# Rotary pairs exchanged by transfers, and attention scores as two split passes

## The reference

```
h = concat([meta_tokens, x]); h = layer_norm(h)          # 528 positions
for l in range(2):
    c_val, c_glu, c_gate, q, k, v, a_gate, r_x, r_gate = split(h @ w_in[l])
    q, k = partial_rotary(q, pos), partial_rotary(k, pos)   # first 16 of 64 dims
    att = sliding_window_sink_attention(q, k, v, sinks)     # window 128, meta keys seen by all
    y = concat([y_conv, att * silu(a_gate), y_lru])
    h = layer_norm(ALPHA * h + y @ w_out[l])

def partial_rotary(x, pos):                  # half = 8
    x1, x2 = x[..., :8], x[..., 8:16]
    return concat([x1 * cos - x2 * sin, x2 * cos + x1 * sin, x[..., 16:]])

s_meta = einsum("bnqkgd,bmkd->bkgnqm", qb, km) * scale     # real queries, 16 meta keys
s_band = einsum("bnqkgd,bnjkd->bkgnqj", qb, k_band) * scale # and 2 blocks of 128 keys
s_mm   = einsum("bqkgd,bmkd->bkgqm", qmg, km) * scale       # meta queries, meta keys
```

## Time and profile before

| | us |
|---|---|
| median of 3 runs (lowest, highest) | 3177.31 (3176.45, 3180.64) |
| the profiled execution's own time | 3175.3 |
| its span | 3173.8 |
| TensorE busy | 3113.7 (98%) |
| VectorE busy | 2194.8 (69%) |
| ScalarE busy | 1557.4 (49%) |
| GpSimd busy | 335.5 (11%) |

### The profile page before, as it was taken

How to read it: one execution, slowest core, us unless ns; L and a number is a source line. 1 busy time by engine, 2 the same in 40 slices (tenths; PEclk the granted TensorE clock), 3 DMA queues, 4 the chain that set the end, 5 groups by cost and what they waited for, 6 DMA issues and landing times.

```text
span 3173.8 us, 59919 instructions
## 1 busy us (share of the span) xinstructions
PE 3113.7 (98%) x23211; PEld 2918.5 (92%) x23211; DVE 2194.8 (69%) x2897; ACT 1557.4 (49%) x2538; POOL 335.5 (11%) x343
## 2 busy tenths in 40 slices
PE   8999999999999999999989999999999999999998
PEld 7899999999999998998889999999998888888898
DVE  7678888888888888786774655566557556556535
ACT  5355555555555555442264554555226455555421
POOL 1000000000000000000001342250000224313000
PEclk9999999999999999999999999999999999999999
DMA  6334444443443435452243222223325322222432
GB/s 209 91 99 108 111 109 113 127 108 103 112 109 102 119 105 180 132 164 93 93 155 98 81 71 71 74 82 122 102 84 169 92 74 80 81 78 70 160 99 88
DMA packets 461729, 342.81 MB, mean 108 GB/s; under 512 B 20505, under 2 KB 451545, under 8 KB 458353
## 3 DMA queue, kind: packets, MB, share of 16 engines
q1 hardware_dynamic: 443712, 296.28, 32.5%
q0 software_dynamic: 8304, 26.92, 2.4%
q10 hardware_dynamic: 9552, 17.37, 1.6%
HBM read 315.04 MB, written 25.46 MB: 107 GB/s over the span
## 4 chain that ended last, share of the span: by engine, by line
PE 75%; DVE 9%; DVEq 5%; DMA 4%; issue 3%; ACT 3%; SPq 0%; ACTq 0%
PE ps L762 13%; PE ps L763 13%; PE ps L764 13%; PE ps L933 5%; PE ps L935 5%; PE ps L936 5%; DVE w_low_blocks L2203 3%; DMA w_raw_blocks<-in_w_in 2%; PE ps L1186 2%; PE ps L1347 1%; PE ps L1345 1%; PE ps L1349 1%; PE ps L768 1%; PE ps L1003 1%; PE ps L769 1%
## 5 line engine op out<-in xcount | busy, mean ns | idle before, releaser
L762 PE MATMUL ps<-x_high,w_high 128*128 128x264 f32 (+3 forms) x2880 | 914.1, 317 | 19.2 <-DVE x_low L2595 10.7
L763 PE MATMUL ps<-x_low,w_high 128*128 128x264 f32 (+3 forms) x2880 | 882.6, 306 | 0.0
L764 PE MATMUL ps<-x_high,w_low 128*128 128x264 f32 (+3 forms) x2880 | 882.4, 306 | 0.0
L2113 DVE TENSOR_TENSOR w_low<-w_raw,w_high 128x1024 fp32r<-128x1024 f32 x308 | 377.7, 1232 | 331.8 <-ACT w_high L1387 317.2
L762 PEld LDWEIGHTS ps<-x_high,w_high 128*128 128x128 f32 x2880 | 544.1, 189 | 51.1 <-issue 21.6
L763 PEld LDWEIGHTS ps<-x_low,w_high 128*128 128x128 f32 x2880 | 544.1, 189 | 28.0 <-issue 3.3
L764 PEld LDWEIGHTS ps<-x_high,w_low 128*128 128x128 f32 x2880 | 542.7, 188 | 25.2
L933 PE MATMUL ps<-x_high_rows,w_high_blocks 128*128 128x256 f32 x1815 | 505.1, 280 | 2.9 <-DVE v_gelu_feature_major L2236 1.9
L935 PE MATMUL ps<-x_low_rows,w_high_blocks 128*128 128x256 f32 x1792 | 496.4, 277 | 0.0
L936 PE MATMUL ps<-x_high_rows,w_low_blocks 128*128 128x256 f32 x1792 | 495.2, 276 | 0.0
L1387 ACT ACTIVATE w_high<-w_raw 128x1024 fp32r<-128x1024 f32 x308 | 324.7, 1056 | 276.3 <-PE ps L764 201.3
(11 more groups left out here) (523 smaller groups left out, 5334.7 us busy)
## 6 DMA issues: line engine op xcount, KB each, us to landing
w_raw_blocks<-in_w_in SPq DMA_DIRECT2D x200, 512.0 KB, 5.1
w_raw<-in_w_in SPq DMA_DIRECT2D x384, 256.0 KB, 3.2
w_raw<-in_w_out SPq DMA_DIRECT2D x224, 256.0 KB, 3.0
w_raw_blocks<-in_w_out SPq DMA_DIRECT2D x24, 512.0 KB, 5.5
residual<-residual_stream ACTq DMA_DIRECT2D x8, 1056.0 KB, 9.7
residual_stream<-y_layer ACTq DMA_DIRECT2D x2, 2176.0 KB, 11.3
x_natural<-in_x SPq DMA_DIRECT2D x4, 1024.0 KB, 9.4
x_feature_major<-x_stage POOLq DMA_DIRECT2D x4, 1024.0 KB, 7.8
```

What stands on the lines that cost most here:

```text
L762: pe.matmul(dst, wh[:, j, kt, wc], x_hi[:, k, tok], start=first, stop=False)
L763: pe.matmul(dst, wh[:, j, kt, wc], x_lo[:, k, tok], start=False, stop=False)
L764: return pe.matmul(dst, wl[:, j, kt, wc], x_hi[:, k, tok], start=False, stop=last)
L2113: dve.tensor_tensor(wl[:, j], raw[:, j], f(wh[:, j]), ALU.subtract).then_inc(lo_ready, 1)
```

## The change

**Rotary.** The product with `rotation` goes, with its constant, for keys and queries. After each copy of queries (or keys) out of PSUM, ScalarE issues four transfers of 8 partitions each, within SBUF, which exchange the rows of each pair into `swapped_pairs`; the sign is now in the sin table. VectorE's `rope` reads that tile in place of PSUM and writes its result to `tmp1` (t = 0) or `c_partial` (t = 1).

**Scores.** For each head, one tile holds the query's high part on the 64 partitions of its own half and its low part on the other half: `q_even_heads` (in the place of the queries) and, for odd heads, `swapped_pairs` (reused). ScalarE writes the high halves (`queries`), VectorE the low halves. The key tile `k_high_low` holds the key's high part on both halves and, in a second plane, its low part on both halves. A score is two float32r passes over the same queries: with the keys' high and with their low plane. ScalarE makes the keys' high parts as before, VectorE 12 subtractions for the low ones between its second and third `low`.

**Order.** TensorE waits for the low halves of the first pair before heads 0 and 1, and of the second pair before heads 2 and 3. VectorE's group loop is written out.

```diff
-        rot = nc.alloc_sbuf_tensor_at("rotation", [P, P], F32, offset=hole + (NM + P) * 4)
-        kz = rr.take("k_zero_padded", [P, 2, 3, NM + 2 * BLK])
+        ks = rr.take("k_high_low", [P, 2, 3, NM + 2 * BLK], F32R)
...
+        swr = rw.take("swapped_pairs", [P, 2, L], F32R)
+        qst = (nc.alloc_sbuf_tensor_at("q_even_heads", [P, 2, L], F32R, offset=big),
+               swr)
+        swap = swr[:].bitcast(F32)
...
+        roped = (t1, cacc)
...
-                pool.dma_start(rot[:], consts[:, K_ROT:K_MASK0]).then_inc(shape_in, 16)
...
-                    def rotate(t):
...
-                        for q, c in enumerate(parts):
-                            last = pe.matmul(ps[:, 4 + 2 * t + q, 0:c.stop - c.start], rot[:], qrw[:, t, c], start=True, stop=True)
-                        last.then_inc(rot_mm, 1)
...
+                    def score(i, n):
+                        q = qst[i % 2][:, i // 2, :]
+                        bank = 4 + n % 2
+                        if n == 0 and i % 2 == 0:
+                            pe.wait_ge(stack_low, 3 * G + i // 2 + 2)
...
-                        last = pe.matmul(ps[:, bank, 0:w], q[:, tq:tq + BLK], kz[:, i % 2, max(n - 1, 0), 0:w],
-                                         start=True, stop=True)
+                        for m in range(2):
+                            last = pe.matmul(ps[:, bank, 0:w], q[:, tq:tq + BLK], ks[:, m, max(n - 1, 0), 0:w],
+                                             start=(m == 0), stop=(m == 1))
...
+                act.wait_ge(zeros_ok, l + 1)
+                act.wait_ge(evac, 2 * (U + O_K2) + 2)
+                for o in (0, PAIR, HD, HD + PAIR):
+                    d = o ^ PAIR
+                    act.dma_start(swap[d:d + PAIR, :, :], krw[o:o + PAIR, :, :]).then_inc(pairs_swapped[0], 16)
...
+                    def swap_pairs(t):
+
+                        act.wait_ge(evac, 2 * V + t + 1)
+                        for o in (0, PAIR, HD, HD + PAIR):
+                            d = o ^ PAIR
+                            act.dma_start(swap[d:d + PAIR, t, cc], qrw[o:o + PAIR, t, cc]).then_inc(pairs_swapped[t], 16)
+
+                    def queries(t):
+
+                        act.wait_ge(rope_done, 2 * G + t + 1)
+                        for h in range(2):
+                            o = h * HD
+                            last = act.activation(qst[h][o:o + HD, t, cc], roped[t][o:o + HD, cc], ACT.Copy)
+                        last.then_inc(stack_high, 1)
...
                     take(V, 0, cols(qrw[:, 0, :]), banks(0))
+                    swap_pairs(0)
                     high(V + 1, 0)
                     values()
                     high(V + 1, 1)
                     keys(0)
-                    keys(1).then_inc(kz_ready, 1)
+                    keys(1).then_inc(stack_high, 1)
                     high(V + 1, 2)
                     take(V, 1, cols(qrw[:, 1, :]), banks(2))
+                    swap_pairs(1)
                     high(V + 1, 3)
+                    queries(0)
+                    queries(1)
...
-                with dve.Fori(0, NKV) as g:
+                for g in range(NKV):
...
-                        dve.wait_ge(rot_mm, 2 * G + t + 1)
-                        dve.tensor_tensor(cols(t1[:]), banks(4 + 2 * t), cols(sin), ALU.mult)
+                        dve.wait_ge(pairs_swapped[t], 64 * (G + 1 + (l + 1 if t == 0 else 0)))
+                        dve.tensor_tensor(r[:, cc], swap[:, t, cc], sin[:, cc], ALU.mult)
...
+                    def queries(t):
+
+                        dve.wait_ge(stack_high, 3 * G + t + 2)
+                        for h in range(2):
+                            o, d = h * HD, (1 - h) * HD
+                            last = dve.tensor_tensor(qst[h][d:d + HD, t, cc], roped[t][o:o + HD, cc],
+                                                     f(qst[h][o:o + HD, t, cc]), ALU.subtract)
+                        last.then_inc(stack_low, 1)
...
+                            for e in range(3):
+                                dve.tensor_tensor(z[:, e, NM:], k[:, NM + e * BLK:NM + (e + 2) * BLK], f(hi_k[:, e, NM:]), ALU.subtract)
+                            for e in range(3):
+                                last = dve.tensor_tensor(z[:, e, 0:NM], k[:, 0:NM], f(hi_k[:, e, 0:NM]), ALU.subtract)
...
-                    lows(V + 1)
+                    low(V + 1, 0)
+                    low(V + 1, 1)
+                    keys()
+                    low(V + 1, 2)
+                    low(V + 1, 3)
                     rope(0)
                     rope(1)
+                    queries(0)
+                    queries(1)
...
-            c[o + q:o + q + half, K_SIN:K_ALL] = np.sin(ang).T
+            c[o + q:o + q + half, K_SIN:K_ALL] = np.sin(ang).T if q else -np.sin(ang).T
```

More of the change, by code:

```diff
@@ L50 @@
 HD = 64
+PAIR = HD // 4 // 2
 NKV = 4
@@ L115 @@
 OUT_ORDER = (6, 7, 0, 1, 2, 3, 4, 5)
-K_IDENT, K_ONES, K_TRI, K_ROT = 0, P, 2 * P, 3 * P
-K_MASK0 = 4 * P
+K_IDENT, K_ONES, K_TRI = 0, P, 2 * P
+K_MASK0 = 3 * P
 K_MASK = K_MASK0 + NM + BLK
@@ L1143, in _ @@
                 unit_half(U + O_K2, fill, COLS[1], (1, 2), hook=parameters)
[L1145 to L1155, removed]
+                unit(U + O_GRP, fill, wide=True, real=(real, real))
                 def group(g, ending=None):
@@ L1160, in group @@
                     A = NH * l + GROUP * g
-                    def rotate(t):
-                        if t == 0:
-                            pe.wait_ge(evac, 2 * V + 2)
-                            pe.wait_ge(k_roped, 2 * (l + 1))
+                    def score(i, n):
[3 more added lines that the diff above has]
+                            pe.wait_ge(stack_low, 3 * G + i // 2 + 2)
+                        if n == 0 and i == 0:
+                            pe.wait_ge(pl_ok, l + 1)
                             pe.wait_ge(r_act, 2 * G)
-                            pe.wait_ge(o_taken, 2 * G)
                             if not real:
                                 pe.wait_ge(mo_ready, 2 * G)
-                        for q, c in enumerate(parts):
-                            last = pe.matmul(ps[:, 4 + 2 * t + q, 0:c.stop - c.start], rot[:], qrw[:, t, c], start=True, stop=True)
-                        last.then_inc(rot_mm, 1)
[L1176 to L1181, removed]
                         pe.wait_ge(s_taken, 4 * A + 4 * i + n + 1)
@@ L1185, in score @@
                         w = NM + (2 if n else 1) * BLK
-                        last = pe.matmul(ps[:, bank, 0:w], q[:, tq:tq + BLK], kz[:, i % 2, max(n - 1, 0), 0:w],
-                                         start=True, stop=True)
+                        for m in range(2):
+                            last = pe.matmul(ps[:, bank, 0:w], q[:, tq:tq + BLK], ks[:, m, max(n - 1, 0), 0:w],
+                                             start=(m == 0), stop=(m == 1))
                         if n == 0 and not real:
-                            last = pe.matmul(ps[:, bank, 160:160 + NM], q[:, 0:BLK], kz[:, i % 2, 0, 0:NM],
-                                             start=True, stop=True)
+                            for m in range(2):
+                                last = pe.matmul(ps[:, bank, 160:160 + NM], q[:, 0:BLK], ks[:, m, 0, 0:NM],
+                                                 start=(m == 0), stop=(m == 1))
                         last.then_inc(s_done, 1)
@@ L2802, in _ @@
                     dve.drain()
-                    dve.wait_ge(rotk_mm, 2 * l + m + 1)
-                    dve.tensor_tensor(two(t1[:]), halves(4 + 2 * m), two(sin), ALU.mult)
+                    dve.tensor_tensor(t1[:], swap[:, m, :], sin, ALU.mult)
                     dve.tensor_tensor(k, k, cos, ALU.mult)
@@ new lines, in keys @@
+                    def keys():
+                        dve.wait_ge(stack_high, 3 * G + 1)
+                        own = slice(g % 2 * HD, g % 2 * HD + HD)
+                        k = krw[own, g // 2, :]
+                        hi_k = ks[own, 0]
+                        for h in range(2):
+                            z = ks[h * HD:(h + 1) * HD, 1]
+                            for e in range(3):
+                                dve.tensor_tensor(z[:, e, NM:], k[:, NM + e * BLK:NM + (e + 2) * BLK], f(hi_k[:, e, NM:]), ALU.subtract)
+                            for e in range(3):
+                                last = dve.tensor_tensor(z[:, e, 0:NM], k[:, 0:NM], f(hi_k[:, e, 0:NM]), ALU.subtract)
+                        last.then_inc(stack_low, 1)
@@ L3072, in shape_constants @@
     c[:, K_TRI:K_TRI + P] = i[:, None] <= i[None, :]
-    half = HD // 4 // 2
-    for o in (0, HD):
-        for d in range(half):
-            c[o + half + d, K_ROT + o + d] = -1.0
-            c[o + d, K_ROT + o + half + d] = 1.0
     neg = np.float32(-1e30)
@@ L3085, in shape_constants @@
     c[:, K_CAUS:K_COS] = own[:, 0:NM]
+    half = PAIR
     freq = np.float32(500000.0) ** (-np.arange(half, dtype=np.float32) / np.float32(half))
```

24 lines of the change are left out of this document (12 added, 12 removed).

## The result

| | before | changed |
|---|---|---|
| median (lowest to highest), 11 runs each on one chip | 3177.94 us (3175.92 to 3181.06) | 3185.86 us (3182.36 to 3188.23) |
| ratio to before, 95% interval | | 1.0022 (1.0014 to 1.003) |
| span of the profiled execution | 3173.8 us | 3182.8 us |

The kernel became slower by 0.2%; 3163 was forecast, with a range that ended at 3174. TensorE has less to do and the time is longer, so it must stand still more.

A forecast was written before the change was run, and what follows sets the result against it. TensorE, 98% busy, was taken as the bound: gains of 9.0 (six later groups), 8.6 (first groups) and 3.6 (keys' rotation), 21.2 us, less 7.7 for narrow scores, 13.5; forecast 3163 us, range 3157 to 3169, wider 3149 to 3174.

The forecast's parts named there:

- the issue's time: On ScalarE's queue, each small transfer's issue takes 0.42 us; four with the wait on their copy take 1.8 us.
- rival 4: Nothing gained: issues of 0.6 us and key subtractions without overlap give 3179 us; chance 0.12.
- the first groups: Each layer's first group has no recurrence ahead; the added work fits with 0.9 us to spare, both keep 4.3 us gain.
- The chain behind the issues: In six later groups, ScalarE's issues delay w_high, w_low, rotations and low halves: first score 1.0 us later, net 1.5 gained.
- The keys' subtractions: VectorE's 12 subtractions per group take 2.3 us overlapped; the third w_low then comes late, a TensorE stall of 0.8 us.
- Narrow scores: The 32 scores of 144 columns go from 0.24 to 0.48 us as two passes each: 7.7 us lost.
- Rival 1: Narrow score passes cost only their weight loads: 3154 us on the profile, 3156 in the runs; chance 0.27.
- Wide scores: The 96 scores of 272 columns go from 0.46 to 0.25 us as two passes each: 20.2 us saved.
- rival 3: Exchanged pairs land late, so VectorE's rotations wait for transfers and eight first scores slip: 3200 us; chance 0.07.

The follow-up runs named there:

- e7: The changed kernel with the queries' transfers issued by SyncE and only the keys' four, once a layer, by ScalarE: 3149.79 us, ratio 0.9899 to before.
- e6: The changed kernel with transfers issued by SyncE and VectorE taking the first pair's low halves before the second pair's rotation: 3143.94 us, ratio 0.988 to before.
- e1: The changed kernel with its 72 transfers issued by SyncE between its weight loads instead of by ScalarE: 3145.09 us, ratio 0.9893 to before.
- e8: The changed kernel with each of ScalarE's two batches of issues put behind the next w_high conversion instead of ahead: 3159.91 us, ratio 0.9928 to before.

## Why the prediction was wrong

**The step that failed first is the issue's time: 0.42 us taken, 0.63 measured.** It came from a load of a constant and seven residual loads, all reading the chip's memory; these transfers go from on-chip memory to on-chip memory. Which of their differences makes them dearer no run shows. Four took 2.62 to 2.64 us and held the row 2.75 to 2.78, where 1.8 was put down. Two batches: 5.5 for 3.6. I had the dearer value as rival 4 with 0.12 and the range ended below its time.

This alone is not the whole miss: by my own sum it is 6 x 1.9 = 11.4 us, 3174 for 3163. **Two terms were put at nothing:** the waits of the first groups, which have 2.4 us each and not "0.9 to spare", and the clock, 8.5 us; I priced a wait at its own length.

- *The chain behind the issues* was right, link by link. I measure from ScalarE's first copy of queries (1809.23 before, 1808.42 after). The last w_low should have ended 1822.75 - 1809.23 = 13.5 us behind it and ended 1822.88 + 1.23 - 1808.42 = 15.7 behind it. Rotations: 4.4 for 4.6. First low halves: 1.45 for 1.3. The first score came at 21.6 against 1828.6 - 1809.23 = 19.4 forecast and 18.4 before: 3.2 later instead of 1.0, and 3.1 to 3.3 later in all six groups that follow another. Of the 2.2 too much the issues are 1.9.
- *The keys' subtractions* took 2.75 for 2.3. They did not delay the first score, since the fourth w_low waited 1.39 for ScalarE anyway. But the third w_low stands behind them and ends at 1821.50, and TensorE waits 1.29 for it; 0.8 was forecast.
- *The first groups:* the layer's start has the keys' batch ahead of everything (3.29 us), which I left out of that sum. e7 shows that this alone is covered.
- *V+1's first piece* was a place I didn't look at: the first batch stands ahead of its w_high. 5.6 us in six groups. These waits and those for w_low are not lost on top of the chain: the first score comes when ScalarE and VectorE are ready for it, and what TensorE waits at these earlier places it waits less at the score.
- *Narrow scores:* wrong bound. In e6, where nothing waits, the two 144-column passes start at 1825.87 and the 16-column ones 0.18 later, where the earlier trace rows had 0.24. But the passes behind them pay for it: the second projection matmul follows at 1826.44, 0.57 behind the first narrow pass, where it was 1712.23 - 1711.64 = 0.59 before. So 0.02 is gained for such a place, about 32 x 0.02 = 0.6 us in all, not 7.7 lost. Rival 1, nothing gained and nothing lost, was right, and without this error the forecast would have been further off; that it brought the forecast nearer is luck. Right after the idle time the 144-column pair took 0.28 (1830.03 to 1830.31).

```profile
1825.87 0.34 PE L1199 MATMUL ps<-k_high_low,q_even_heads 128*128 128x144 f32 x2
1826.05 0.33 PE L1203 MATMUL ps<-k_high_low,q_even_heads 128*128 128x16 f32 x2
1826.23 0.37 PE L793 MATMUL ps<-x_high,w_high 128*128 128x264 f32 x1
1826.44 0.28 PE L794 MATMUL ps<-x_low,w_high 128*128 128x264 f32 x1
```

- *Wide scores:* 0.25 forecast. The 272-column score at 1716.16 is followed by the next projection matmul at 1716.41: 0.25 (TensorE of the changed kernel).

```profile
1716.16 0.41 PE L1175 MATMUL ps<-k_high_low,q_even_heads 128*128 128x272 f32 x2
1716.41 0.28 PE L769 MATMUL ps<-x_high,w_high 128*128 128x264 f32 x1
```

- *Landing* (rival 3) never came in: with e6 the rotation starts right behind w_low, and no wait for a transfer is among TensorE's. VectorE waits for one once, 0.6 us at the keys.

The sum again, from the landmark, by what was wrong. Forecast -13.5. The six later groups 6 x 2.2 = 13.2 more; the first groups 2 x (2.4 + 0.16 at the wait's start) = 5.1 more; the clock 8.5; the transposes 2.2; the narrow scores 7.7 + 0.6 = 8.3 less. That makes +7.2, and +7.0 was measured.

I should have weighed a rule that speaks for another version: the Trainium skill ("Perfetto Trace Analysis", section "DMA Optimizations") says that where making the transfers' descriptors is the bottleneck, and not the data's way, it may help to balance them over the engines that can issue. e1 agrees: 1.29 points for a change of queue.

## What to carry to other kernels

A transfer's price has two parts, the issuing engine's time and the landing, and here the first was the one that counted: take it from an issue of the same kind (source, destination, partitions), and if there is none, keep the dearer end inside the range. Before adding issues to an engine, find who waits for its next instruction; put them on an engine that has the time, or behind a long operation that somebody waits for, never ahead of it. And a wait of more than two microseconds on TensorE, in a stretch that was dense before, is to be priced with a spell at the lower clock, 1.7 us in five cases of eight here. When you read a pass's price from the next start, look at the start after that too: part of the price can stand there.

## What the runs showed of the hardware that I had not expected

- An issue between two on-chip tiles takes 0.63 us on ScalarE's queue and 0.62 to 0.66 on SyncE's (e6), for 16.5 KB. The keys' transfers are twice as large (33 KB) and in the changed kernel took hardly longer in the median, 0.66:

```profile
L1862 ACTq DMA_DIRECT2D swapped_pairs<-k_roped x8: 631/663/1250, 1677.0 to 2472.9; - x8
```

- Issues run beside a ScalarE operation in flight (e8), so only what sticks out behind it delays the next: 1.77 us of 2.64.
- With 2.3 to 2.5 us of idling the granted clock went to its lower level for about 3.4 us, in five groups of eight. It fell at no fixed time: 1.8 us after the work resumed in one (1948.83), 1.2 in two (1830.03, 2505.85), 0.2 in one (2619.48), and 0.3 before it in the last (2845.20), by windows of half a microsecond. With passes in place of the idle time it fell in no group. Why three groups were spared isn't known.
- A split pass of 272 columns takes 0.125 us. Passes of 144 and 16 columns, each with its own weight load, take 0.11 on the average: four of them and the projection matmul behind take the 0.57 above, no less per pass than the 0.11 from one transpose to the next.
